# Opening of a two-model transformer kernel: products of zeros in the waits, squares summed half by half, modulation pieces two chunks ahead

## The chip, the cores and the metric

The kernel runs on one core of one Trainium2 chip, in one launch. The metric is the device time of a run in microseconds; lower is better. A core has five engines that run their own instruction lists and meet through semaphores: TensorE (PE) multiplies matrices, VectorE (DVE) and ScalarE (ACT) work element by element, GpSimd (POOL) does element work and issues transfers, SyncE (SP) issues transfers.

## The reference

A float32 network for one sequence of 256 tokens and a context of 256 tokens, width 1024. Two layers of a first model (feed-forward, mixing, feed-forward, each behind an RMS norm that is modulated by shift and scale) and two layers of a second model follow. The change touches only what precedes the first feed-forward product:

```python
def rms_norm(x, gain=None):
    xf = x.astype(jnp.float32)
    y = xf * lax.rsqrt(jnp.mean(xf * xf, axis=-1, keepdims=True) + EPS)
...
def modulate(h, shift, scale):
    return h * (1.0 + scale) + shift
def swiglu(h, w1, w3, w2):
    return (jax.nn.silu(h @ w1) * (h @ w3)) @ w2
```

Shift and scale are slices of silu(c) @ w_mod + b_mod for the tokens, and of silu(c_ctx) @ w_mod + b_mod for the context. For the first norm these are 2 x 1024 columns of the first layer's w_mod.

## The kernel before, in words

Activations are kept transposed: 8 chunks of 128 channels on the partitions, 512 columns (256 tokens of x, then 256 of the context). Every float32 weight is multiplied as a high and a low part. A "unit" is 128x1024 of weights. Six ring slots take units from HBM; ScalarE copies a unit rounded into `high` (line 1363, four slots), VectorE subtracts that from it into `low` (line 1864), and `product` (lines 808 to 810) makes three products per 128x128 block. `split_ahead` in both engines' lists keeps the splitting up to four units ahead of TensorE.

The opening (`start_units`) runs as follows.

- POOL issues x in two halves, the context in two halves, then the eight 1 MB pieces of `w_mod_first` (line 726, four slots; piece c holds the shift and scale columns of chunk c) with ring units 0 and 1 behind piece 0 and ring unit 2 behind piece 2. From piece 4 on it waits until TensorE has read the piece four before. SP issues units 3 and on when piece 7 has landed.
- ScalarE squares x and context, four chunks at a time (line 1806). VectorE adds eight chunks of squares to one in three steps per half (lines 2554, 2557, 2560), and TensorE sums them over the partitions with one product per half (lines 937 and 942) into the bank `means`. ScalarE takes the inverse root (lines 1370, 1373).
- For each chunk c: `first_modulation(c)` (line 906, 16 records) multiplies piece c; `first_rows(c)` copies the result out of PSUM on ScalarE (line 1782); `first_turn(c)` (line 915) sums and turns it into columns; `first_shift_scale(c)` (line 2524) and `first_scaled(c)` (line 2536) on VectorE; `first_high(c)` (line 1792) on ScalarE; `first_low(c)` (line 2546) on VectorE. Then `part(i, c)` multiplies chunk c into unit i, i being 0, 1 or 2.

The order is written out by hand in each engine's list. TensorE has: modulation c, part(2, c - 3), turn c, part(0, c - 1), part(1, c - 1). ScalarE has: rows c, high c, with the splitting of unit 2 behind high 1. VectorE has: shift and scale c, scaled c, low c, again with the splitting of unit 2 behind chunk 1. Behind the eight chunks comes the rest of the first feed-forward, a plain loop over units.

Of the kernel before, what the change touches and what calls it, by code (L numbers as in the profile page):

```python
# [32 lines left out]
ALU = mybir.AluOpType  # L33
# [25 lines left out]
FIRST_SLOTS = 4  # L59

# [158 lines left out]
def build(nc, A, old=None):  # L219
    ev = Events(*(old or (None, None)))  # L220
    ctx = ExitStack()
    with ctx:
# [101 lines left out]
        fresh = sb("fresh", 2 * N1).rearrange("p (b n) -> p b n", b=2)  # L324
        narrow = sb("narrow", N2 + 8 * NARROW)
# [282 lines left out]
        def _(pool):  # L608
# [114 lines left out]
            for c in range(KC):  # L723
                if c >= FIRST_SLOTS:
                    pool.wait_ge(*when("first_mod", c - FIRST_SLOTS))
                pool.dma_start(first_mod[:, c % FIRST_SLOTS], A["w_mod_first"][c].rearrange("p (k n) -> p k n", k=KC)).then_inc(
                    *made(f"first_mod_loaded{c % FIRST_SLOTS}", c, by=16))
                for s in ((0, 1), (), (2,))[c] if c < 3 else ():
                    pool.dma_start(ring[:, s], A["stream"][s]).then_inc(*made(f"first_unit_loaded{s}", s, by=16))
# [45 lines left out]
        def _(pe):  # L775
# [123 lines left out]

            def first_modulation(c):  # L900
# [18 lines left out]
            def start_units(tag, keys, xh, xl):  # L919
# [4 lines left out]
                def part(i, c):  # L924
# [9 lines left out]
                means = take("mean", ("start",))  # L934
                pe.wait_ge(*when("consts_loaded", 0))
                pe.wait_ge(*when("first_sums", 0))
                pe.matmul(means[:, 0:NX], cst(C_ONESD), sumsq[:, 0:NX], start=True, stop=True)
                pe.wait_ge(*when("c_cols_silu", 0))
                first_modulation(0)
                first_turn(0)  # L940
                pe.wait_ge(*when("first_sums", 1))
                pe.matmul(means[:, NX:N1], cst(C_ONESD), sumsq[:, NX:N1], start=True, stop=True).then_inc(
                    *made("mean", ("start",)))
                for c in range(1, KC):
                    first_modulation(c)
                    if c >= 3:
                        part(2, c - 3)
                    first_turn(c)
                    part(0, c - 1)
                    part(1, c - 1)  # L950
                pe.wait_ge(*when("consts_loaded_rest", 0))
                for i, c in ((2, 5), (0, 7), (1, 7), (2, 6), (2, 7)):
                    part(i, c)
# [393 lines left out]
        def _(act):  # L1347
# [463 lines left out]
            inverse_root(rstd[:, 0], bank("mean", ("start",)), N1, ("start",), ("mean", ("start",)))  # L1811
            first_high(0)
            split_ahead(1)
            for c in range(1, KC):
                first_rows(c)
                first_high(c)
                if c == 1:
                    split_ahead(1)
# [34 lines left out]
        def _(dve):  # L1853
# [661 lines left out]

            dve.memset(c_wide, 0.0).then_inc(*made("c_wide_cleared"))
# [34 lines left out]
            for g in range(2):  # L2551
                a, b = norm_cols(("start",), g)
                dve.wait_ge(*when("first_squares", g, 1))
                dve.tensor_tensor(scaled[:, 0:4, a:b], scaled[:, 0:4, a:b], scaled[:, 4:8, a:b], ALU.add).then_inc(
                    *made("first_sum_steps", "first_fours", g))
                dve.wait_ge(*when("first_sum_steps", "first_fours", g))
                dve.tensor_tensor(scaled[:, 0:2, a:b], scaled[:, 0:2, a:b], scaled[:, 2:4, a:b], ALU.add).then_inc(
                    *made("first_sum_steps", "first_twos", g))
                dve.wait_ge(*when("first_sum_steps", "first_twos", g))
                dve.tensor_tensor(sumsq[:, a:b], scaled[:, 0, a:b], scaled[:, 1, a:b], ALU.add).then_inc(  # L2560
                    *made("first_sums", g))
# [6 lines left out]
            for c in range(1, KC):  # L2568
# [3 lines left out]
                if c == 1:  # L2572
                    split_ahead(1)
# [173 lines left out]
```

## Time and profile before

| | |
|---|---|
| median of 3 runs | 2410.36 us (2410.29 to 2411.43) |
| the profiled execution, its own time | 2411.78 us |
| its span | 2409.5 us |
| TensorE busy | 2354.6 us (98%) |
| VectorE busy | 1537.7 us (64%) |
| ScalarE busy | 1012.7 us (42%) |
| GpSimd busy | 402.2 us (17%) |
| HBM read | 357.34 MB |

The profile is of one execution. Its span runs from the first to the last instruction; the time of the run is a little longer. In the timeline a row gives the start in us, the duration in us, engine, line, operation, what is written and read, and how often; brackets give the idle time of the engine before it and what ended that. PEld is TensorE's weight load, which overlaps its products. Ends of products are modelled, so consecutive ones overlap in the rows; their starts tell the pace.

### The profile page before, as it was taken

Reading aid. Unit: us, or ns where it says so; the run is one execution under the profiler, and the core shown is the slowest. Engines: PE = TensorE matmul, PEld = TensorE weight load, DVE = VectorE, ACT = ScalarE, POOL = GpSimd, SP = SyncE. Lnnn points to the kernel's source line nnn. Section 1 sums busy time; section 2 is a strip of 40 time slices with the busy share of each in tenths; the row PEclk is TensorE's granted clock in tenths of the full one; section 3 lists DMA queues with packets and bytes.
Section 4 is the critical chain, followed back from the end, with each engine's and each line's share of the span. In section 5 each row is a group of like instructions: output and inputs, shape, how many; then the busy total and the mean of one; then the engine's idle time right before and its main releaser. Section 6 shows DMA issues by size and latency. Waiting matters only on the chain.

```text
span 2409.5 us, 36413 instructions
## 1 busy us (share of the span) xinstructions
PE 2354.6 (98%) x14350; PEld 2038.1 (85%) x14350; DVE 1537.7 (64%) x2616; ACT 1012.7 (42%) x1690; POOL 402.2 (17%) x425
## 2 busy tenths in 40 slices
PE   7999999999999999999999999999999999999998
PEld 4888888777888888888888877999888999899887
DVE  5888775884698865523323585766666665667874
ACT  5222224645522223422223465555445444446663
POOL 2221211240122221111011131121000120000110
PEclk9999999999999999999999999999999999999999
DMA  8555542112366664222222222555433555434553
GB/s 341 193 208 207 186 158 90 62 53 93 114 219 235 238 217 157 88 96 97 96 97 99 87 80 76 188 184 188 156 106 127 172 175 175 148 117 152 190 189 135
DMA packets 97864, 360.75 MB, mean 150 GB/s; under 512 B 11024, under 2 KB 11792, under 8 KB 96544
## 3 DMA queue, kind: packets, MB, share of 16 engines
q1 hardware_dynamic: 75744, 272.84, 32.6%
q0 software_dynamic: 21952, 85.59, 9.8%
q8 instruction: 115, 1.88, 0.3%
q14 instruction: 53, 0.43, 0.1%
HBM read 357.34 MB, written 1.05 MB: 149 GB/s over the span
## 4 chain that ended last, share of the span: by engine, by line
PE 90%; DVE 3%; ACT 3%; issue 2%; DMA 1%; POOL 0%; DVEq 0%; ACTq 0%; POOLq 0%
PE bank L808 25%; PE bank L810 24%; PE bank L809 24%; PE bank L815 6%; PE bank L816 3%; PE bank L1143 1%; ACT ring_high L1363 1%; PE bank L1131 1%; PE bank L1113 1%; DVE ring_low L1864 1%; PE bank L1165 1%; PE bank L1092 0%; DMA arena<-w_mod_first_dram 0%; PE bank L1312 0%; PE bank L906 0%
## 5 line engine op out<-in xcount | busy, mean ns | idle before, releaser
L1864 DVE TENSOR_TENSOR ring_low<-ring,ring_high 128x1024 fp32r<-128x1024 f32 x520 | 641.2, 1234 | 509.1 <-ACT ring_high L1363 506.7
L808 PE MATMUL bank<-x_parts,ring_high 128*128 128x512 f32 (+2 forms) x2308 | 801.8, 347 | 6.9 <-DVE x_parts L1939 3.7
L1363 ACT ACTIVATE ring_high<-ring 128x1024 fp32r<-128x1024 f32 x520 | 547.9, 1054 | 582.0 <-PE bank L810 541.9
L810 PE MATMUL bank<-x_parts,ring_low 128*128 128x512 f32 (+2 forms) x2308 | 788.1, 341 | 0.0
L809 PE MATMUL bank<-x_parts,ring_high 128*128 128x512 f32 (+2 forms) x2308 | 786.6, 341 | 0.0
L808 PEld LDWEIGHTS bank<-x_parts,ring_high 128*128 128x128 f32 x2308 | 436.4, 189 | 73.6 <-issue 14.4
L809 PEld LDWEIGHTS bank<-x_parts,ring_high 128*128 128x128 f32 x2308 | 436.8, 189 | 47.0 <-issue 1.0
L810 PEld LDWEIGHTS bank<-x_parts,ring_low 128*128 128x128 f32 x2308 | 436.3, 189 | 47.6
L640 POOL TENSOR_TENSOR hidden_parts<-fresh,hidden_parts 128x512 fp32r<-128x512 f32 (+2 forms) x132 | 205.0, 1553 | 1013.1 <-ACT hidden_parts L1496 1013.1
L1877 DVE CUSTOM_DVE_ANT_0 mod_products<-mod_ring,csilu 128x1024 bf16<-128x1024 f32 x224 | 300.9, 1379 | 30.5 <-DMA mod_ring<-w_mod_dram 29.6
L808 PE MATMUL bank<-hidden_parts,ring_high 128*128 128x512 f32 (+2 forms) x814 | 280.9, 345 | 0.8 <-POOL hidden_parts L640 0.8
L810 PE MATMUL bank<-hidden_parts,ring_low 128*128 128x512 f32 (+2 forms) x814 | 280.1, 344 | 0.0
L809 PE MATMUL bank<-hidden_parts,ring_high 128*128 128x512 f32 (+2 forms) x814 | 280.1, 344 | 0.0
L808 PEld LDWEIGHTS bank<-hidden_parts,ring_high 128*128 128x128 f32 x814 | 153.6, 189 | 19.5 <-POOL hidden_parts L640 1.3
L809 PEld LDWEIGHTS bank<-hidden_parts,ring_high 128*128 128x128 f32 x814 | 153.6, 189 | 18.1
L810 PEld LDWEIGHTS bank<-hidden_parts,ring_low 128*128 128x128 f32 x814 | 153.6, 189 | 18.1
L1485 ACT ACTIVATE act_out<-bank 128x512 f32<-128x512 f32 x66 | 39.5, 599 | 264.6 <-PE bank L810 264.6
L815 PE MATMUL bank<-x_parts,ring_high 128*128 128x512 f32 x352 | 123.2, 393 | 0.0
L815 PE MATMUL bank<-hidden_parts,ring_high 128*128 128x512 f32 x308 | 106.9, 392 | 0.0
L808 PE MATMUL bank<-early_parts,ring_high 128*128 128x258 f32 x352 | 99.9, 284 | 0.0
L810 PE MATMUL bank<-early_parts,ring_low 128*128 128x258 f32 x352 | 99.3, 282 | 0.0
L809 PE MATMUL bank<-early_parts,ring_high 128*128 128x258 f32 x352 | 99.3, 282 | 0.0
(264 smaller groups left out, 2738.5 us busy)
## 6 DMA issues: line engine op xcount, KB each, us to landing
ring<-stream_dram SPq DMA_DIRECT2D x517, 512.0 KB, 3.3
mod_ring<-w_mod_dram POOLq DMA_DIRECT2D x128, 512.0 KB, 4.4
arena<-w_mod_first_dram POOLq DMA_DIRECT2D x8, 1024.0 KB, 10.3
ring<-stream_dram POOLq DMA_DIRECT2D x3, 512.0 KB, 10.8
arena<-na_bias_dram POOLq DMA_DIRECT2D x2, 768.0 KB, 11.0
mod_ring<-consts_dram POOLq DMA_DIRECT2D x1, 1076.0 KB, 5.1
resid<-x_dram POOLq DMA_DIRECT2D x2, 512.0 KB, 6.0
resid<-ctx_dram POOLq DMA_DIRECT2D x2, 512.0 KB, 7.2
```

The source lines that it names most:

```text
L640: pool.tensor_tensor(lo[:, f], fresh[:, f % 2, 0:n], hi[:, f].bitcast(F32), ALU.subtract).then_inc(*made("hidden_low", tag, h, f))
L808: pe.matmul(out, w[0][:, b], xh, start=start, stop=False)
L809: pe.matmul(out, w[0][:, b], xl, start=False, stop=False)
L810: return pe.matmul(out, w[1][:, b], xh, start=False, stop=stop)
L815: pe.matmul(bank.rearrange("p (k n) -> p k n", k=2), w[0][:, b], both, start=start, stop=False)
L816: return pe.matmul(bank[:, 0:NX], w[1][:, b], high, start=False, stop=stop)
L1113: mm = pe.matmul(out, pr["q"][r, q:q + nq], pr["k"][r, 0:NZ if twin else nk], start=not fox, stop=True, skip_group_check=nq < P)
L1131: mm = pe.transpose(p[0:rows, kt * P:kt * P + nq], probs[0:nq, b, e, kt * P:kt * P + rows], cst(C_IDENT, nq, nq))
L1363: act.activation(high[:, i % SPLIT], ring[:, u % LOADED], ACT.Copy).then_inc(high_parts, 1)
L1485: act.activation(act_out[:, f % 2, 0:n], p[:, 0:n], ACT.Silu).then_inc(*made("silu", tag, h, f, frees=("gate", tag, h, f)))
L1864: dve.tensor_tensor(low[:, u % LOADED], ring[:, u % LOADED], high_f[:, i % SPLIT], ALU.subtract).then_inc(low_parts, 1)
L1877: dve.tensor_tensor_reduce(junk[:, s], mod_ring[:, n % MOD_RING], csilu[:, s], 1.0, 0.0, ALU.mult, ALU.add, mod[:, l, s, j:j + 1]).then_in ...
```

## The change

`zeros` is the second half of `fresh[:, 1]`, set to zero by VectorE's first instruction. `idle_products(count, key)` waits for an event and then multiplies zeros by zeros into bank 4, `count` times. They are put ahead of and between the sums and the first two modulations. The squares are added from four chunks to two on VectorE, one add for each half and each four chunks, and TensorE sums the remaining pairs itself, eight products accumulated in `means`. On TensorE modulation and turn run two chunks ahead of the parts, and `first_rows` on ScalarE moves accordingly; the splitting of unit 2 moves behind chunk 2. Ring unit 1 is issued behind piece 1 and ring unit 2 behind piece 3.

```diff
--- before.py
+++ after.py
@@ -57,6 +57,7 @@
 LN_EXP = "natural_log_exp_and_others"
 
 FIRST_SLOTS = 4
+IDLE_BANK = 4
 
 
 
@@ -322,6 +323,7 @@
         act_out = sb("act_out", 2 * N1).rearrange("p (b n) -> p b n", b=2)
         c_wide = act_out[:, 0, 0:KC * 32].rearrange("p (c n) -> p c n", c=KC)
         fresh = sb("fresh", 2 * N1).rearrange("p (b n) -> p b n", b=2)
+        zeros = fresh[:, 1, NX:N1]
         narrow = sb("narrow", N2 + 8 * NARROW)
         row_scale = narrow[:, 0:N2]
         gate_w = narrow[:, 16:16 + 16 * NARROW].rearrange("p (s b n) -> p s b n", s=2, b=8)
@@ -725,7 +727,8 @@
                     pool.wait_ge(*when("first_mod", c - FIRST_SLOTS))
                 pool.dma_start(first_mod[:, c % FIRST_SLOTS], A["w_mod_first"][c].rearrange("p (k n) -> p k n", k=KC)).then_inc(
                     *made(f"first_mod_loaded{c % FIRST_SLOTS}", c, by=16))
-                for s in ((0, 1), (), (2,))[c] if c < 3 else ():
+                if c in (0, 1, 3):
+                    s = min(c, 2)
                     pool.dma_start(ring[:, s], A["stream"][s]).then_inc(*made(f"first_unit_loaded{s}", s, by=16))
             pool.dma_start(resid[:, :, 0:META], A["meta"]).then_inc(*made("meta_loaded", 0, by=16))
             pool.dma_start(const[:, C_ONES64:CONSTS], A["consts"][:, C_ONES64:CONSTS]).then_inc(
@@ -897,6 +900,13 @@
                         for c in order:
                             part(i, c)
 
+            def idle_products(count, *ready):
+
+
+                pe.wait_ge(*when(*ready))
+                for _ in range(count):
+                    pe.matmul(psum[IDLE_BANK][:, 0:NX], zeros[:, 0:P], zeros, start=True, stop=True)
+
             def first_modulation(c):
 
                 p = take_at(5 + c % 2, "first_rows", c)
@@ -932,25 +942,47 @@
                         mm.then_inc(*made(*keys[i], unit=i))
 
                 means = take("mean", ("start",))
+
+                def sums(g, i):
+                    a, b = norm_cols(("start",), g)
+                    pe.wait_ge(*when("first_sums", g, i))
+                    for j in range(2):
+                        mm = pe.matmul(means[:, a:b], cst(C_ONESD), scaled[:, 4 * i + j, a:b],
+                                       start=(i == 0 and j == 0), stop=(i == 1 and j == 1))
+                    return mm
+
+                idle_products(7, "zeros_set")
+                idle_products(2, "x_loaded0", 0)
                 pe.wait_ge(*when("consts_loaded", 0))
-                pe.wait_ge(*when("first_sums", 0))
-                pe.matmul(means[:, 0:NX], cst(C_ONESD), sumsq[:, 0:NX], start=True, stop=True)
+                sums(0, 0)
+                idle_products(1, "ctx_loaded0", 0)
+                sums(0, 1)
+                sums(1, 0)
                 pe.wait_ge(*when("c_cols_silu", 0))
+                idle_products(1, "ctx_loaded1", 1)
                 first_modulation(0)
+                sums(1, 1).then_inc(*made("mean", ("start",)))
                 first_turn(0)
-                pe.wait_ge(*when("first_sums", 1))
-                pe.matmul(means[:, NX:N1], cst(C_ONESD), sumsq[:, NX:N1], start=True, stop=True).then_inc(
-                    *made("mean", ("start",)))
+                idle_products(2, "first_mod_loaded0", 0)
+                first_modulation(1)
+                idle_products(1, "first_mod_loaded1", 1)
+                first_turn(1)
+                part(0, 0)
+                first_modulation(2)
+                part(1, 0)
+                first_turn(2)
                 for c in range(1, KC):
-                    first_modulation(c)
-                    if c >= 3:
-                        part(2, c - 3)
-                    first_turn(c)
-                    part(0, c - 1)
-                    part(1, c - 1)
+                    part(0, c)
+                    part(1, c)
+                    if c + 2 < KC:
+                        first_modulation(c + 2)
+                    if c >= 2:
+                        part(2, c - 2)
+                    if c + 2 < KC:
+                        first_turn(c + 2)
                 pe.wait_ge(*when("consts_loaded_rest", 0))
-                for i, c in ((2, 5), (0, 7), (1, 7), (2, 6), (2, 7)):
-                    part(i, c)
+                part(2, KC - 2)
+                part(2, KC - 1)
 
             def begun(prev):
 
@@ -1809,12 +1841,15 @@
             split_ahead(1 - SPLIT)
             act.wait_ge(*when("mean", ("start",)))
             inverse_root(rstd[:, 0], bank("mean", ("start",)), N1, ("start",), ("mean", ("start",)))
+            first_rows(1)
             first_high(0)
             split_ahead(1)
+            first_rows(2)
             for c in range(1, KC):
-                first_rows(c)
                 first_high(c)
-                if c == 1:
+                if c + 2 < KC:
+                    first_rows(c + 2)
+                if c == 2:
                     split_ahead(1)
             for l in range(DEPTH):
                 t1, tm, to, t2 = ("ffn1", l), ("mix1", l), ("out1", l), ("ffn2", l)
@@ -2513,6 +2548,7 @@
                     if k < len(PROJ2):
                         project(tp, PROJ2, k, N2, proj2, VTEMP2)
 
+            dve.memset(zeros, 0.0).then_inc(*made("zeros_set"))
             dve.memset(c_wide, 0.0).then_inc(*made("c_wide_cleared"))
             dve.memset(eps_one[:, 0:1], EPS).then_inc(*made("eps_one", 0))
             dve.memset(eps_one[:, 1:2], 1.0).then_inc(*made("eps_one", 1))
@@ -2550,15 +2586,10 @@
 
             for g in range(2):
                 a, b = norm_cols(("start",), g)
-                dve.wait_ge(*when("first_squares", g, 1))
-                dve.tensor_tensor(scaled[:, 0:4, a:b], scaled[:, 0:4, a:b], scaled[:, 4:8, a:b], ALU.add).then_inc(
-                    *made("first_sum_steps", "first_fours", g))
-                dve.wait_ge(*when("first_sum_steps", "first_fours", g))
-                dve.tensor_tensor(scaled[:, 0:2, a:b], scaled[:, 0:2, a:b], scaled[:, 2:4, a:b], ALU.add).then_inc(
-                    *made("first_sum_steps", "first_twos", g))
-                dve.wait_ge(*when("first_sum_steps", "first_twos", g))
-                dve.tensor_tensor(sumsq[:, a:b], scaled[:, 0, a:b], scaled[:, 1, a:b], ALU.add).then_inc(
-                    *made("first_sums", g))
+                for i in range(2):
+                    dve.wait_ge(*when("first_squares", g, i))
+                    x = scaled[:, 4 * i:4 * i + 4, a:b]
+                    dve.tensor_tensor(x[:, 0:2], x[:, 0:2], x[:, 2:4], ALU.add).then_inc(*made("first_sums", g, i))
             dve.wait_ge(*when("small_loaded", 0))
             first_shift_scale(0)
             split_ahead(1 - SPLIT)
@@ -2569,7 +2600,7 @@
                 first_shift_scale(c)
                 first_scaled(c)
                 first_low(c)
-                if c == 1:
+                if c == 2:
                     split_ahead(1)
             split_ahead(1)
             for l in range(DEPTH):
```

## Rows read from the trace of the kernel before

**Rows 1.** Page: the chain that ended last, shares of the span by engine.

```profile
PE 90%; DVE 3%; ACT 3%; issue 2%; DMA 1%; POOL 0%; DVEq 0%; ACTq 0%; POOLq 0%
```

**Rows 2.** Waits of TensorE from 50 us on: total, times, longest.

```profile
PE bank L1281 <- DVE fresh L2134: 4.4, 2, 2.3
```

**Rows 3.** Windows: busy us and instructions of each engine, granted clock, DMA share, GB/s.

```profile
12.00:28.80 16.80, 12.75 (x66) 6.41 (x66) 10.16 (x18) 7.32 (x13) 1.21 (x3) 1.00 1.01 416
28.80:54.00 25.20, 24.66 (x172) 17.10 (x173) 15.30 (x42) 10.62 (x20) 7.08 (x13) 1.00 0.91 353
54.00:90.00 36.00, 36.00 (x160) 29.84 (x159) 32.05 (x42) 14.71 (x20) 9.82 (x9) 1.00 0.56 203
```

**Rows 4.** Timeline, end of the opening: start, us, engine, line, operands, idle before.

```profile
49.69 0.88 DVE L2546 SCALAR_TENSOR_TENSOR x_parts<-arena,mod,x_parts 128x256 fp32r<-128x256 f32 x2 [0.24 <-ACT x_parts L1792]
...
50.72 0.47 PE L808 MATMUL bank<-x_parts,ring_high 128*128 128x512 f32 x1 [0.42 <-DVE x_parts L2546]
...
53.56 0.39 PE L808 MATMUL bank<-x_parts,ring_high 128*128 128x512 f32 x1
```

**Rows 5.** Timeline, modulation 2, while slow.

```profile
26.39 1.94 PE L906 MATMUL bank<-arena,act_out 128*32 128x256 f32 x16
```

**Rows 6.** Timeline, one chunk (4) once fast.

```profile
34.65 1.07 PE L906 MATMUL bank<-arena,act_out 128*32 128x256 f32 x16
...
35.79 0.38 ACT L1782 ACTIVATE fresh<-bank 128x256 f32<-128x256 f32 x1 [0.65 <-PE bank L906]
...
36.83 0.48 PE L808 MATMUL bank<-x_parts,ring_high 128*128 128x512 f32 x1
...
37.00 0.35 DVE L2524 TENSOR_SCALAR mod<-bank,small 128x2 f32<-128x2 f32 x2 [1.34 <-PE bank L915]
...
37.97 0.91 ACT L1792 ACTIVATE x_parts<-arena,mod 128x256 fp32r<-128x256 f32 x2 [1.80 <-DVE arena L2536]
...
38.39 1.07 PE L906 MATMUL bank<-arena,act_out 128*32 128x256 f32 x16
...
38.51 0.89 DVE L2546 SCALAR_TENSOR_TENSOR x_parts<-arena,mod,x_parts 128x256 fp32r<-128x256 f32 x2 [0.24 <-ACT x_parts L1792]
```

**Rows 7.** Timeline, 10 to 14 us.

```profile
10.79 0.69 DVE L2557 TENSOR_TENSOR arena<-arena 128x512 f32<-128x512 f32 x1
11.27 1.06 ACT L1806 ACTIVATE arena<-resid 128x1024 f32<-128x1024 f32 x1 [0.36 <-DMA resid<-ctx_dram]
...
12.09 1.19 PE L937 MATMUL bank<-sumsq,const 128*128 128x256 f32 x2 [12.09 <-DVE sumsq L2560]
...
13.86 1.94 PE L906 MATMUL bank<-arena,act_out 128*32 128x256 f32 x16 [0.58 <-DMA arena<-w_mod_first_dram]
```

**Rows 8.** Timeline, 18 to 30 us.

```profile
18.40 0.69 ACT L1370 ACTIVATE rstd<-bank,eps_one 128x512 f32<-128x512 f32 x1 [1.22 <-PE bank L942]
...
18.80 1.93 PE L906 MATMUL bank<-arena,act_out 128*32 128x256 f32 x16 [0.44 <-DMA arena<-w_mod_first_dram]
...
19.86 0.88 DVE L2536 SCALAR_TENSOR_TENSOR arena<-resid,mod,rstd 128x256 f32<-128x256 f32 x2 [0.96 <-ACT rstd L1373]
...
23.55 0.77 PE L808 MATMUL bank<-x_parts,ring_high 128*128 128x512 f32 x1
...
25.50 1.04 ACT L1363 ACTIVATE ring_high<-ring 128x1024 fp32r<-128x1024 f32 x1
...
26.58 1.23 DVE L1864 TENSOR_TENSOR ring_low<-ring,ring_high 128x1024 fp32r<-128x1024 f32 x1 [0.46 <-ACT ring_high L1363]
...
29.36 0.47 PE L808 MATMUL bank<-x_parts,ring_high 128*128 128x512 f32 x1
```

**Rows 9.** Timeline of TensorE around its longest idle time but one.

```profile
1723.03 0.63 PE L1281 MATMUL bank<-fresh,mod_ring 128*8 128x272 f32 x2 [2.10 <-DVE fresh L2134]
...
1723.82 0.29 PE L809 MATMUL bank<-x_parts,ring_high 128*128 128x272 f32 x1
1723.94 0.28 PE L810 MATMUL bank<-x_parts,ring_low 128*128 128x272 f32 x1
```

## The prediction, written before the result was known

> **What bounds the kernel now.** I read the page's chain of waits first, then the busy shares, then the waits of TensorE after the opening. The chain lies on TensorE for 90% of the span [rows 1], and behind 54 us it stands still only in small pieces, the largest group being 4.4 us [rows 2]. From 54 to 90 us it is busy without a break [rows 3]. VectorE is nearly full there too (32.05 of 36 us), but it splits a weight unit some units before TensorE multiplies it, so it doesn't set the pace. No row shows anything there that waits for a fixed time. So whatever the opening wins or loses reaches the end one for one, and the question is when TensorE leaves the opening. Before, the first product of unit 3, which follows the last of the opening, starts at 53.56 [rows 4].
>
> The opening itself has two parts. [...] From 29 us on it is busy for 24.66 of 25.2 us: each chunk costs 3.74 us (modulation of one chunk starts at 34.65, of the next at 38.39) [rows 6], and that is TensorE's own work.
>
> **The start, up to the first product of chunk 1.** On VectorE three adds per half, in a row, go (the middle one took 0.69 us [rows 7], the first has twice its size, the last half of it) and two of the middle size per half come, so VectorE has less to do. The last square ends at 11.27 + 1.06 = 12.33 [rows 7], so its add ends near 13.1. Added on TensorE: eight products of 128x256 for the sums in place of two, and 14 products of zeros. A product of this form appears as two records, 1.19 us with its tail when cold [rows 7]; I take 0.85 us apart when cold, 0.43 warm. The memset of zeros has the size of one that is there for `c_wide`; it delays ScalarE's table loads by some tenths, and the squares wait for their transfers well behind those (the last starts at 11.27 [rows 7]), so it costs nothing. The first nine idle products run from 1.3 to between 7 and 9 us, beside the transfers of x; the sums of the first three halves and their two fillers fit before 13.9 if the clock is up by then (three sums of 0.87, two fillers of 0.43; the last starts at about 11.8). I take it that it is up: nine products without a gap are some 7 us of work, and in the trace the clock was still low at 26.39 and came up behind that, after products that began at 23.55 [rows 5, 8].
>
> Then, with the clock up:
> - Modulation 0 still waits for its transfer, at 13.86 [rows 7]. ScalarE copies its rows 1.14 us behind it (34.65 to 35.79 [rows 6]), 15.0, and splits unit 0 (1.04 for such a split [rows 8]) until 16.4. The last sum (0.87) ends at 15.8, hidden by that. The root starts at 16.4, where it was 18.40, and 1.46 us later (18.40 to 19.86 [rows 8]) VectorE scales chunk 0: 17.9.
> - Modulation 1 is loaded earlier: one ring unit (0.52 MB) is now behind it in POOL's queue, at the 416 GB/s of this stretch [rows 3] 1.3 us, so at 17.5 in place of 18.80 [rows 8]. Here the first cost appears: `first_rows(1)` stands ahead of `first_high(0)` on ScalarE, so it waits for modulation 1: 17.5 + 1.14 = 18.64, and high 0 starts at 18.9, not at 18.4. Low follows 0.54 later (37.97 to 38.51), and the first product 1.03 behind the low's start (49.69 to 50.72) [rows 4, 6]: 20.5, before 23.55 [rows 8].
> - Unit 1 is split on ScalarE from 19.8 and on VectorE from 20.9 to 22.1; only then comes shift 1, with 0.97 from it to the high (37.00 to 37.97), then low and product: the first product of chunk 1 at 24.6. Before: 29.36 [rows 8]. So 4.8 us are won here.
>
> Queues that the edit passes: ring unit 1 lands where modulation 1 did, 18.8, for a split at 19.8: 1 us of cover, and what is lost of it moves chunk 1. Ring unit 2 is at about 25, needed at 32. Modulations 4 to 7 are issued as their slots come free, earlier than before; modulation 4 by bytes (5.8 MB behind piece 0 at 416 GB/s) at 27.7, needed at 30.8; later ones have more room. SP's stream starts when piece 7 has landed, sooner than before; unit 3 is needed only behind 53, so this is worth nothing.
>
> **The loop over the chunks.** TensorE's order is now: two groups of products of chunk c (units 0 and 1), modulation c + 2, the third unit's group of chunk c - 2, turn c + 2. The work is the same 3.7 us. But ScalarE's order is high c, rows c + 2, high c + 1, and rows in the trace come in program order. So high c + 1 waits for modulation c + 2, which TensorE starts only behind its groups of chunk c, which need low c. That closes a loop: groups 0 and 1 of a chunk until the modulation starts, 1.56 us (36.83 to 38.39); modulation to rows 1.14; rows to the next instruction 0.3; high to low 0.54; low to product 1.03 [rows 4, 6]. Sum 4.57 us per chunk, against 3.74. Behind the modulation TensorE has 1.0 + 0.89 + 0.34 of work and then stands for about 0.8 us. Before, high c waited for modulation c in the same way, but behind that modulation TensorE still had both groups of chunk c - 1 to do, some 1.5 us, and these covered it.
>
> At chunk 2 it is worse. The split of unit 2 follows rows 4, so it too waits for modulation 4; VectorE waits for it behind low 2, and shift, scale and low of chunk 3 queue behind. From modulation 4: 1.14 + 0.3 + split to low split 1.08 (25.50 to 26.58 [rows 8]) + its own 1.15 + shift to high 0.97 (37.00 to 37.97 [rows 6]) + 0.54 + 1.03 = 6.2, with the 1.56 before it 7.8 us from chunk 2 to chunk 3. TensorE stands for some 2.8 us of it before the third unit's first group. Before, this split sat in the slow stretch, ahead of modulation 2.
>
> Sum from the first product of chunk 1: 4.57 (to 2) + 7.75 (to 3) + 3 x 4.57 (to 6) + 2.4 (to 7, where no modulation is left: VectorE's own round of a chunk, 0.88 for the low, then 0.97 + 0.54 [rows 6]) + the five groups left, 15 products at 0.23 (TensorE's 12 from 50.72 to 53.56 give 0.237 [rows 4]) = 3.5. That is 31.9 us, where before it took 53.56 - 29.36 = 24.2. Lost here: 7.7. Won before: 4.8. TensorE leaves the opening at 56.5 instead of 53.6, **3.0 us later**.
>
> [...] No row here shows an instruction passing another.
>
> **Against the runs.** The profiled execution took 2411.78 us (span 2409.5), the median 2410.36. So 2414.8 profiled, and by the median 2413.4. 3.0 us are 0.12%; 0.2% (4.8 us) is about what can be told from no change.
>
> **Rivals.**
> - *The clock doesn't come up early* (9 us of products of zeros aren't enough). Then they only stand in the way: nine at 0.85 until 9.0, sums and fillers until 15.9, modulation 0 at 15.9 instead of 13.86, the sum in front of the turn 1.7, three more fillers 2.6, modulations at 1.94. The first product of chunk 1 comes near 31, at worst 1.7 later than before, and with the 7.7 of the loop that is +9.2: 2419.6. It decides if the clock rises behind 16 us (from there the loss is over 5). For it: from 12 to 28 us a TensorE with 12.75 us of work in 16.8 stayed slow [rows 3]. Against it: that work was broken by waits again and again, and the first nine products of zeros follow each other without one. A part of it is a clock that falls again in the 2.8 us stand of chunk 2; against that, products behind an idle time of 2.10 us still come 0.12 us apart, at 272 columns the fast level [rows 9]. It would add 1 to 3 us. [...]
> - *The loop is hidden and the start's gain stays*: TensorE bound at 3.74 from 24.6: 24.2 us on, end at 48.8, -4.8 us, 2405.6. It needs high c + 1 not to wait for rows c + 2. The code's order excludes it nearly; a half way case (delays shorter than I read them, 0.3 us per chunk, and the split of unit 2 landing in the loop) gives -1 to +1.
> - *The transfers set the start*: pieces 1 and 2 land 1.3 us later than by bytes (my bound is the old 18.80). Then chunk 1 is 1.3 us later: +4.3, 2414.7.
>
> **Chances.** Forecast with its own range of +1 to +4.7: 0.62. Slow clock, wholly or in part: 0.17, nearly all of it above +4.8 us. Hidden loop or half way: 0.13, of which 0.07 is beyond -4.8 us. Late transfers: 0.08, half of it above +4.8. Of the forecast's own 0.62 some 0.04 lies above too. Faster by over 0.2%: 0.07; within: 0.69; slower: 0.24. The range leaves out the wholly hidden loop and a little of the cold case: 2409.0 to 2419.5.
>
> **What would show it.** Idle products from 1.3 us, their records 0.43 apart in the start at first, then 0.2; modulation 0 at 13.9 lasting 1.07; scale of chunk 0 at 17.9; first product at 20.5, of chunk 1 at 24.6. In the loop: ScalarE's high always directly behind rows, modulations 4.6 us apart for pieces 5 to 7, TensorE idle 0.8 us before each first group and 2.8 us at 32, ended by VectorE's low part. First product of unit 3 at 56.5. I am wrong if modulations come 3.7 us apart, or if the sixteen products at 13.9 still take 1.9 us.

## The result, and the profile after

The changed kernel took 2417.19 us in the median of 11 runs (2414.21 to 2419.87), the kernel before 2410.74 in the 11 runs beside it (2409.95 to 2413.45): +6.4 us, ratio 1.0023, 95% interval 1.0015 to 1.0030. The prediction was 2413.4 with a range of 2409.0 to 2419.5. So the time lies in the range and on the side forecast, but the loss is twice the 3.0 us of the sum, and above the forecast's own +1 to +4.7. The profiled execution took 2414.21 (span 2412.0) and is the fastest of the eleven; that matters below. One run of the kernel before in a slow state (2911.7 us at a granted clock of 0.753, beside the f experiments) is left out of every figure.

The start went as worked out. First the timeline of TensorE in the changed kernel up to the first product of chunk 1, whose counterpart before was at 29.36 [rows 8]:

```profile
1.19 7.00 PE L908 MATMUL bank<-fresh 128*128 128x256 f32 x18 [1.19 <-DVE fresh L2551]
...
13.84 1.07 PE L916 MATMUL bank<-arena,act_out 128*32 128x256 f32 x16 [0.64 <-DMA arena<-w_mod_first_dram]
...
17.61 1.07 PE L916 MATMUL bank<-arena,act_out 128*32 128x256 f32 x16 [0.32 <-DMA arena<-w_mod_first_dram]
...
20.58 0.47 PE L811 MATMUL bank<-x_parts,ring_high 128*128 128x512 f32 x1 [0.73 <-DVE x_parts L2582]
...
24.57 0.47 PE L811 MATMUL bank<-x_parts,ring_high 128*128 128x512 f32 x1 [0.82 <-DVE x_parts L2582]
```

The 18 records in the first row are nine products of zeros, 7.0 us. Modulation 0 lasts 1.07 us, where it lasted 1.94 [rows 7]: the clock is up. Chunk 0 starts at 20.58 (20.5 forecast), chunk 1 at 24.57 (24.6).

Then the loop and the stand (the long wait of TensorE at chunk 2), first on TensorE and then on ScalarE (start, us, engine, what):

```profile
26.13 1.07 PE L916 MATMUL bank<-arena,act_out 128*32 128x256 f32 x16
...
29.11 0.47 PE L811 MATMUL bank<-x_parts,ring_high 128*128 128x512 f32 x1 [0.73 <-DVE x_parts L2582]
...
30.65 1.07 PE L916 MATMUL bank<-arena,act_out 128*32 128x256 f32 x16
...
34.42 0.80 PE L811 MATMUL bank<-x_parts,ring_high 128*128 128x512 f32 x1 [2.71 <-DVE ring_low L1899]
35.02 0.63 PE L812 MATMUL bank<-x_parts,ring_high 128*128 128x512 f32 x1
...
36.82 0.77 PE L811 MATMUL bank<-x_parts,ring_high 128*128 128x512 f32 x1
...
39.64 1.64 PE L916 MATMUL bank<-arena,act_out 128*32 128x256 f32 x16
...
44.75 1.07 PE L916 MATMUL bank<-arena,act_out 128*32 128x256 f32 x16
...
49.26 1.07 PE L916 MATMUL bank<-arena,act_out 128*32 128x256 f32 x16
...
54.54 0.47 PE L811 MATMUL bank<-x_parts,ring_high 128*128 128x512 f32 x1
...
58.05 0.39 PE L811 MATMUL bank<-x_parts,ring_high 128*128 128x512 f32 x1
```

```profile
31.78 0.38 ACT L1814 ACTIVATE fresh<-bank 128x256 f32<-128x256 f32 x1 [3.34 <-PE bank L916]
32.06 1.05 ACT L1395 ACTIVATE ring_high<-ring 128x1024 fp32r<-128x1024 f32 x1
...
45.88 0.39 ACT L1814 ACTIVATE fresh<-bank 128x256 f32<-128x256 f32 x1 [3.34 <-PE bank L916]
46.16 0.90 ACT L1824 ACTIVATE x_parts<-arena,mod 128x256 fp32r<-128x256 f32 x2
```

The second fence is ScalarE: the split of unit 2 starts right behind rows 4, and a high right behind rows 6, each after 3.34 us of waiting for TensorE's modulation. TensorE in turn stands 0.73 us before a chunk and 2.71 us before the third unit's first group, released by unit 2's low part. Modulations are 4.52 us apart from chunk to chunk (26.13 to 30.65, 44.75 to 49.26), against 3.74 before [rows 6]. All this is the forecast. What isn't: the row at 35.02 takes 0.63 us and the modulation at 39.64 takes 1.64. The clock has fallen in the stand. The windows say it too (us, busy time of PE, PEld, DVE, ACT, POOL, granted clock, DMA share, GB/s):

```profile
28.80:54.00 25.20, 20.08 (x124) 13.45 (x125) 11.18 (x32) 6.80 (x16) 5.45 (x11) 0.86 0.88 348
33.00:35.00 2.00, 0.58 (x1) 0.50 (x2) 1.82 (x4) 0.11 (x1) 1.25 (x3) 0.76 1.02 334
35.00:37.00 2.00, 1.90 (x8) 1.64 (x7) 1.68 (x6) 0.91 (x2) 0.00 (x0) 0.50 0.99 386
37.00:39.00 2.00, 2.00 (x5) 1.60 (x6) 0.98 (x3) 0.00 (x0) 0.00 (x0) 0.50 1.02 407
```

In the first of these stretches the clock before was 1.00 [rows 3]. (The column says 1.00 from 12 to 28.8 us before as well, where modulation 2 takes 1.94 us [rows 3, 5]; there only the durations show that TensorE is slow.) At a granted clock of 0.50 the products of 512 columns start 0.43 us apart (37.38 to 37.81), at 1.00 they start 0.23 us apart (29.41 to 29.64). Chunk 3 started at 36.82 and chunk 4 at 43.21: 6.4 us in place of 4.6. The last chunk starts at 54.54, five groups of three products follow, and the first product of unit 3 comes at 58.05, before at 53.56 [rows 4]: 4.5 us later in this execution, where 3.0 were forecast. From the first product of chunk 1 the chunks take 4.5, 7.7, 6.4, 4.5, 4.5 and 2.3 us and the five groups 3.5; the forecast's terms were 4.57, 7.75, three times 4.57, 2.4 and 3.5. One term is off by more than 0.1 us, that of the slow stretch, by 1.8.

The span is only 2.5 us longer. The lag of 4.5 us holds until 633 us; behind that the clock falls in both executions now and then (granted 0.83 from 630 to 640 and from 1410 to 1420 us before, 0.83 from 1000 to 1010 and 0.81 from 1726 to 1735 in the changed kernel), and TensorE waited 0.7 and 0.6 us less at two places that the change doesn't touch.

### The profile page after: what moved, and what is told of

Read it like the earlier page. It is cut to its first block, busy times and chain, and to the rows that moved or that the text cites. A ratio compares the mean times of both kernels' runs of the same rounds, so it can differ in the third digit from the quotient of the medians.

```text
span 2412.0 us, 36492 instructions
## 1 busy us (share of the span) xinstructions
PE 2364.8 (98%) x14390; PEld 2047.0 (85%) x14390; DVE 1535.9 (64%) x2615; ACT 1012.6 (42%) x1690; POOL 400.3 (17%) x425
## 4 chain that ended last, share of the span: by engine, by line
PE 89%; DVE 4%; ACT 3%; issue 2%; DMA 1%; POOL 0%; DVEq 0%; ACTq 0%; POOLq 0%
PE bank L811 25%; PE bank L813 24%; PE bank L812 24%; PE bank L818 6%; PE bank L819 3%; ACT ring_high L1395 1%; PE bank L1175 1%; DVE ring_low L1899 1%; PE bank L1163 1%; PE bank L1145 1%; PE bank L1197 1%; DMA arena<-w_mod_first_dram 0%; PE bank L1124 0%; PE bank L1344 0%; DVE arena L1965 0%
```

## The experiments

Each was timed beside the kernel before, in three groups: e1, e2, e3 and e5 (median of before 2411.40), e4, e6, e7 and e8 (2411.94), and f1 to f4 (2411.64). The table gives the difference from that median and the ratio with its 95% interval, which is some 2 us to either side for eleven runs. A difference between two kernels of the table is therefore sure to some 2.7 us (an estimate: two such intervals, added as squares). The last column is the start of the first product of unit 3, the first behind the opening, in the profiled execution (before: 53.56).

| kernel | median, us | against before, us | ratio | unit 3, us |
|---|---|---|---|---|
| changed | 2417.19 | +6.4 | 1.0023 (1.0015 to 1.0030) | 58.05 |
| e1_split_first | 2410.94 | -0.5 | 1.0000 (0.9991 to 1.0008) | 52.96 |
| e2_high_first | 2407.01 | -4.4 | 0.9986 (0.9977 to 0.9994) | 49.41 |
| e3_fill_stand | 2414.18 | +2.8 | 1.0015 (1.0006 to 1.0024) | 57.53 |
| e4_no_idle (5 runs) | 2421.21 | +9.3 | 1.0038 (1.0024 to 1.0052) | 63.13 |
| e5_idle_only | 2408.04 | -3.4 | 0.9989 (0.9981 to 0.9998) | 51.42 |
| e6_high_first_no_idle | 2409.26 | -2.7 | 0.9988 (0.9979 to 0.9997) | 50.80 |
| e7_old_order | 2410.05 | -1.9 | 0.9992 (0.9983 to 1.0000) | 50.95 |
| e8_squares_only | 2410.40 | -1.5 | 0.9993 (0.9984 to 1.0002) | 54.67 |
| f1_fill_gaps | 2407.16 | -4.5 | 0.9984 (0.9975 to 0.9992) | 49.43 |
| f2_old_order_ring | 2406.85 | -4.8 | 0.9984 (0.9975 to 0.9993) | 49.20 |
| f3_chunk1_early | 2406.47 | -5.2 | 0.9980 (0.9971 to 0.9989) | 49.15 |
| f4_high_first_split_late | 2411.33 | -0.3 | 1.0000 (0.9991 to 1.0008) | 53.40 |

**The stand: e1_split_first.** On ScalarE, against the changed kernel:

```diff
                 first_high(c)
+                if c == 2:
+                    split_ahead(1)
                 if c + 2 < KC:
                     first_rows(c + 2)
-                if c == 2:
-                    split_ahead(1)
```

> The changed kernel, with ScalarE's split of unit 2 ahead of rows 4 instead of behind them. My theory: the 2.7 us stand of TensorE at chunk 2 comes from that split waiting for modulation 4, and it also throws the clock down. Then chunk 2 to 3 costs 4.55 us like the others, the granted clock stays 1.00, and the first product of unit 3 starts at about 53.2 (57.4 in the changed kernel): -0.4 us against before, median about 2410.3. Rival (the loss sits in the transfers or behind the opening): stays at 2415 to 2417.

Measured 2410.94: as the theory says. The place of this split was worth 6.9 us (+6.4 against -0.5, each by its own before). In its timeline of ScalarE the split runs while ScalarE would wait anyway, and the chunks still come 4.5 us apart (rows 3 at 27.16, rows 4 at 31.70):

```profile
27.16 0.38 ACT L1814 ACTIVATE fresh<-bank 128x256 f32<-128x256 f32 x1 [3.36 <-PE bank L916]
27.44 0.90 ACT L1824 ACTIVATE x_parts<-arena,mod 128x256 fp32r<-128x256 f32 x2
28.23 1.04 ACT L1395 ACTIVATE ring_high<-ring 128x1024 fp32r<-128x1024 f32 x1
31.70 0.39 ACT L1814 ACTIVATE fresh<-bank 128x256 f32<-128x256 f32 x1 [2.42 <-PE bank L916]
```

**The loop: e2_high_first.** As the one before, and:

```diff
-                if c + 2 < KC:
-                    first_rows(c + 2)
+                if 2 < c + 1 < KC:
+                    first_rows(c + 1)
```

> As the one before, and on ScalarE high c + 1 ahead of rows c + 2 (the order is high 1, high 2, rows 3, high 3, rows 4, ...). My theory: ScalarE's order closes the loop of 4.55 us per chunk; with it opened TensorE is the bound at 3.73 us per chunk from 24.6 us on, unit 3 starts at about 48.8, -4.8 us against before, 2405.9. Rival (VectorE's chain or the transfers of the pieces set the pace of a chunk, not ScalarE's order): the chunks stay over 4.2 us apart and it ends within 1 us of the first experiment.

Measured 2407.01, -4.4: another 3.9 us. In the traces the five chunks from 1 to 6 take 18.6 us, where e1_split_first took 22.7, and the last one 0.4 us more: 3.7 us. ScalarE's timeline shows the loop open; the high of chunk 3 (29.39) waits for VectorE and stands ahead of rows 4 (30.96), which wait 0.66 us only:

```profile
27.28 0.38 ACT L1814 ACTIVATE fresh<-bank 128x256 f32<-128x256 f32 x1
29.39 0.91 ACT L1824 ACTIVATE x_parts<-arena,mod 128x256 fp32r<-128x256 f32 x2 [1.73 <-DVE arena L2572]
30.96 0.39 ACT L1814 ACTIVATE fresh<-bank 128x256 f32<-128x256 f32 x1 [0.66 <-PE bank L916]
```

**Loop open, stand kept: f4_high_first_split_late.** The same order, but unit 2's split behind rows 4; on ScalarE, against e2_high_first (and on VectorE `c == 3` for `c == 2`):

```diff
-                if c == 2:
-                    split_ahead(1)
                 if 2 < c + 1 < KC:
                     first_rows(c + 1)
+                if c == 3:
+                    split_ahead(1)
```

> The second experiment's order on ScalarE (high c + 1 ahead of rows c + 2), but unit 2's split left behind rows 4 (on VectorE behind low 3): the loop is opened, the stand is kept. From modulation 4 the third unit's first group has to wait 1.14 + 0.3 + 1.08 + 1.3 = 3.8 us, of which 1.0 is the modulation: TensorE stands 2.8 us once, and the later chunks cost 3.73. My theory: 2.8 to 4 us over the second experiment (the upper end if the clock falls in the stand), -0.5 to -1.6 against before. Rival (the stand's price is mostly in the chunks' loop behind it): within 1.5 us of the second experiment.

Measured -0.3, 4.1 over e2_high_first: the upper end. Its profile shows the stand alone, 2.71 us, and a fallen clock from 1 us behind its end (0.63 for the product at 36.05; granted 0.50 from 34.5 to 37.5, 1.00 again from 38). The two faults do not simply add: with the stand in place, opening the loop gained 6.8 us (changed kernel against this one), and without it 3.9. In the changed kernel the clock stayed at 0.50 from 35 to 39 us, and here it was up by 38.

```profile
32.00 1.23 DVE L1899 TENSOR_TENSOR ring_low<-ring,ring_high 128x1024 fp32r<-128x1024 f32 x1 [1.51 <-ACT ring_high L1395]
33.28 0.50 PE L811 MATMUL bank<-x_parts,ring_high 128*128 128x512 f32 x1 [2.71 <-DVE ring_low L1899]
...
36.05 0.63 PE L811 MATMUL bank<-x_parts,ring_high 128*128 128x512 f32 x1
```

**The clock in the stand: e3_fill_stand.**

```diff
+                    if c == 2:
+                        idle_products(5, "zeros_set")
                     if c >= 2:
                         part(2, c - 2)
```

> The changed kernel with five more products of zeros in the stand at chunk 2, ahead of the third unit's first group. The stand stays, as unit 2's low part comes no sooner; only TensorE isn't idle in it. My theory: the part of the loss beyond 3 us is the clock that falls in that stand, so with it filled the clock stays up and it takes about 2413.8, 3.1 over before, with less spread than the changed kernel. Rival (the idle time itself doesn't move the clock, or the spread is from elsewhere): 2417 as the changed kernel.

Measured +2.8 (2414.18), 3.7 less than the changed kernel when each is taken against its own before. Against e1_split_first, measured beside it, it is 3.2 us slower, which is the stand by the forecast's own terms (7.75 - 4.57). The time is what the theory gave. The profile doesn't give its reason as neatly: in this one execution the clock fell as well, for about 3 us (granted 0.50 from 31 to 33) and ahead of the stand, where TensorE had only the loop's pauses of 0.6 to 0.7 us. Modulation 4 is slow, and behind the products of zeros, from 35.74, the products are fast:

```profile
29.84 0.47 PE L811 MATMUL bank<-x_parts,ring_high 128*128 128x512 f32 x1
30.11 0.63 PE L812 MATMUL bank<-x_parts,ring_high 128*128 128x512 f32 x1
30.54 0.63 PE L813 MATMUL bank<-x_parts,ring_low 128*128 128x512 f32 x1
31.10 1.94 PE L916 MATMUL bank<-arena,act_out 128*32 128x256 f32 x16
32.96 2.64 PE L908 MATMUL bank<-fresh 128*128 128x256 f32 x10
35.74 0.50 PE L811 MATMUL bank<-x_parts,ring_high 128*128 128x512 f32 x1
```

So in this execution filling the stand left a short slow stretch; it doesn't keep the clock from falling each time.

**What products of zeros are worth: e4_no_idle, e6_high_first_no_idle, e5_idle_only.** The first two leave them out of the changed kernel and of e2_high_first (the waits stay); the third has nothing but them, added to the kernel before (below the edit of the first two, and of the third on TensorE).

```diff
-                for _ in range(count):
+                for _ in range(0):
```

```diff
+                idle_products(7, "zeros_set")
+                idle_products(2, "x_loaded0", 0)
+                idle_products(1, "ctx_loaded0", 0)
+                idle_products(1, "ctx_loaded1", 1)
                 pe.wait_ge(*when("consts_loaded", 0))
...
+                    if c == 1:
+                        idle_products(2, "first_mod_loaded0", 0)
                     first_modulation(c)
+                    if c == 1:
+                        idle_products(1, "first_mod_loaded1", 1)
```

> The changed kernel without its products of zeros; the waits that stood in front of them stay. My theory: the clock comes up only behind 23 us, modulations 0 and 1 and the sums take twice as long, the first product of chunk 1 comes at about 27.5 in place of 24.6, and the pauses of the loop make it fall or stay low for a part of the chunks too: +3 to +5 us over the changed kernel, 2420 to 2422. Rival (the start waits for transfers, the clock is of no account there): 2417 as the changed kernel.

> The second experiment (unit 2's split early, high c + 1 ahead of rows c + 2) without the products of zeros. If their worth is the same under any order, it takes 3 to 4 us more than the 2407.0 of the second experiment: 2410.5. Rival (with an order that has no pauses the clock comes up by itself nearly as soon): under 1.5 us more, 2408.5 at most.

> The kernel before with the products of zeros alone (14 of them, at the start, in front of and behind modulation 1); order, sums and transfers as before. My theory: the clock comes up before 14 us and that is worth nearly all that the start can win: modulation 2 at 22.6 in place of 26.4, then 3.73 us per chunk: -4.5 us, 2406.2. Rival (the start waits for the transfers and for the sums on VectorE, so a fast clock gives little): -1 us or less.

Without them the changed kernel takes 2421.21, 2.8 more against its own before and just under my +3 to +5, and e2_high_first 2409.26, 1.7 more by the same count (2.3 by the medians), between theory and rival. Neither difference is clear of its uncertainty. Half of my reason was wrong. In e4_no_idle modulation 0 runs fast already, behind the first six products of the sums and nothing else; the clock falls afterwards, in the pauses (granted 0.50 from 20 to 26 us):

```profile
13.95 1.07 PE L916 MATMUL bank<-arena,act_out 128*32 128x256 f32 x16
17.70 1.07 PE L916 MATMUL bank<-arena,act_out 128*32 128x256 f32 x16 [1.28 <-DMA arena<-w_mod_first_dram]
22.22 1.94 PE L916 MATMUL bank<-arena,act_out 128*32 128x256 f32 x16
```

Added to the kernel before they give -3.4, less than the 4.5 expected. In the profiled execution they didn't hold the clock up to modulation 0, with 2.4 us of waits for the context's transfers between them and only two products for the sums; modulations 0 and 1 ran slow, 2 fast, 1.6 us sooner than before [rows 5]:

```profile
13.95 1.93 PE L915 MATMUL bank<-arena,act_out 128*32 128x256 f32 x16 [0.60 <-DMA arena<-w_mod_first_dram]
20.08 1.94 PE L915 MATMUL bank<-arena,act_out 128*32 128x256 f32 x16
24.81 1.07 PE L915 MATMUL bank<-arena,act_out 128*32 128x256 f32 x16
```

**Squares alone: e8_squares_only.** The kernel before with VectorE's two adds per half and, on TensorE:

```diff
-                pe.wait_ge(*when("first_sums", 0))
-                pe.matmul(means[:, 0:NX], cst(C_ONESD), sumsq[:, 0:NX], start=True, stop=True)
+                sums(0, 0)
+                sums(0, 1)
+                sums(1, 0)
                 pe.wait_ge(*when("c_cols_silu", 0))
                 first_modulation(0)
+                sums(1, 1).then_inc(*made("mean", ("start",)))
                 first_turn(0)
-                pe.wait_ge(*when("first_sums", 1))
-                pe.matmul(means[:, NX:N1], cst(C_ONESD), sumsq[:, NX:N1], start=True, stop=True).then_inc(
-                    *made("mean", ("start",)))
```

> The kernel before with the squares summed half by half alone (two adds per half on VectorE, eight products on TensorE, the last two behind modulation 0). My theory: at the slow clock the three sums (1.7 us each) end at 14.1, modulation 0 starts 0.2 us later than before and the last sum takes 1.7 where 0.9 was; the root starts within 1 us of 18.4: -0.5 to +1 us, 2411 to 2412. Rival (more work on TensorE before 14 us brings the clock up by itself): -3 us.

Measured -1.5, with an interval that holds 1. Between theory and rival, and for the rival's reason: modulation 0 took 1.07 us at 13.78 here. It didn't last: in this execution, the slowest of its eleven, modulation 2 took 1.94 us at 24.30.

**Is running two chunks ahead worth anything? e7_old_order, f2_old_order_ring.** The changed kernel's start with the old order in the chunks on all three engines. On TensorE, the prologue of chunks 1 and 2 gone, it is again:

```diff
+                for c in range(1, KC):
+                    first_modulation(c)
...
+                    if c >= 3:
+                        part(2, c - 3)
+                    first_turn(c)
+                    part(0, c - 1)
+                    part(1, c - 1)
```

The second has the ring units issued as before too:

```diff
-                if c in (0, 1, 3):
-                    s = min(c, 2)
+                for s in ((0, 1), (), (2,))[c] if c < 3 else ():
```

> The changed kernel's start (products of zeros, squares half by half, ring units behind pieces 1 and 3) with the order of the kernel before in the chunks on all three engines. My theory: running two chunks ahead is worth nothing by itself, since TensorE is the bound at 3.73 us a chunk in both orders; the start is worth 4 us: modulation 2 at about 23, first product of unit 3 near 49.5, -4.1 us against before, 2407.2, the same as the second experiment. Rival (two chunks ahead helps once ScalarE's order is right): 2 us or more slower than the second experiment, 2409 or more.

> The experiment with the old chunk order, with the ring units issued as before too (0 and 1 behind piece 0, unit 2 behind piece 2). There ScalarE stood 1.8 us for ring unit 2, and rows 2 with turn 2 behind it. If that is why it missed the second experiment by 3 us, it now takes 1.5 us less, 3.5 under before. Rival (the old order loses by the clock that falls at chunk 0, as ring unit 2 only moves one wait into another): no less than 0.5 us better.

The first missed: 2410.05, -1.9, 2.5 us worse than e2_high_first by the same count, as the rival had it. Its profile named a wait, ScalarE's for ring unit 2, which the change moved behind piece 3; rows 2 stand behind that split:

```profile
24.85 1.06 ACT L1388 ACTIVATE ring_high<-ring 128x1024 fp32r<-128x1024 f32 x1 [1.81 <-DMA ring<-stream_dram]
25.82 0.36 ACT L1807 ACTIVATE fresh<-bank 128x256 f32<-128x256 f32 x1
```

With the old places of the ring units it takes 2406.85, -4.8, 2.9 better. That is more than the 1.5 of the wait; in the first the clock also fell behind 21.6 (granted 0.55 from 21.6 to 24), in the second's profile it didn't (1.00), so the rest may be clock. What follows: with each order's transfers right, two chunks ahead shows no gain over the order of before (f1_fill_gaps, measured beside it, is at -4.5).

**What is left: f1_fill_gaps, f3_chunk1_early.** One more product of zeros in each of the three pauses that e2_high_first has left (ahead of part(0, 0), of part(0, 1) and of turn 3), each `+ idle_products(1, "zeros_set")`; the second also has this, on ScalarE `first_high(1)` ahead of `first_rows(2)`, and on VectorE:

```diff
             first_low(0)
+            first_shift_scale(1)
+            first_scaled(1)
             split_ahead(1)
```

> The second experiment (unit 2's split early, high c + 1 ahead of rows c + 2) with one more product of zeros in each of the three pauses left: ahead of chunk 0's first product, ahead of chunk 1's, and ahead of turn 3. My theory: each is shorter than its pause (0.43 against 0.6 to 0.8 us), so nothing gets later, and the clock falls in fewer executions: 0.5 to 1 us under the second experiment, 4.5 to 5.4 under before. Rival (what is left of the spread has another cause): the same as the second experiment, within 0.5 us.

> The first of this call, and chunk 1's shift and scale on VectorE ahead of unit 1's low part, its high on ScalarE ahead of rows 2. My theory: chunk 1's first product starts 0.4 to 0.6 us sooner (at 24.1), TensorE is the bound from there, so 0.5 us under the first of this call, 5 to 6 under before. Rival (unit 1's low part, 0.9 us later, holds back its first group and turn 2 instead): no gain, or 0.3 us slower.

The first shows no gain (-4.5 against -4.4, and three of its eleven runs still have a granted clock of 0.994 and take 2410.3 to 2410.5). The second has the lowest median of all, 2406.47, -5.2; modulation 3 comes at 25.91 where f1_fill_gaps has 26.17. Its lead over its neighbours, 0.4 to 0.7 us, is inside their intervals. It beats both kernels.

## Why the prediction was right, and where its size was off

- *The opening decides, one for one.* Shown: every experiment changes the opening alone, and against before the median moves as the start of unit 3 does, within 1.3 us. Two are further off: the changed kernel (1.9), whose profiled execution is the fastest of its eleven, and e8_squares_only (2.6), whose is the slowest.
- *The start wins 4.8 us.* Shown: 29.36 to 24.57 in the profile, and f2_old_order_ring, which has no loop and starts chunk 1 at 25.02, 4.3 us sooner than before, is 4.8 under before. That the clock comes up through the products of zeros alone was wrong (e4_no_idle, e8_squares_only).
- *The loop of 4.57 us per chunk, closed by ScalarE's order.* Shown: 4.52 in the profile, and e2_high_first opens it for 3.9 us (3.7 in the traces).
- *The stand of 2.8 us.* Shown: 2.71 in the profile; e1_split_first takes it out, and f4_high_first_split_late puts it back into an open loop.
- *The sum, +3.0.* This is the term that was mis-sized: I priced the stand at its idle time and left the clock out of it. By the runs the stand cost 6.9 us (changed against e1_split_first, each with its own before), where the sum had 3.2 (7.75 - 4.57). Filling it with products of zeros gave back 3.7 of these without ending it sooner, and left +2.8, nearly the +3.0 of the sum. I had read the row of 2.10 us of idle time with fast products behind it [rows 9] as safety up to 2.8 us, and put the fall into a rival at 1 to 3 us with small weight. It belongs in the sum. One row was one draw, too: in the changed kernel's own trace the same wait, 2.15 us, has slow products behind it (last section). How much the clock costs depends on what follows the stand: with the loop open the stand cost 4.1 us (f4_high_first_split_late against e2_high_first).
- *The range.* That the time lies in it is in part luck. The forecast's own part went to +4.7 only; the range reached 2419.5 mainly for a clock that doesn't come up at the start, and in the profile it came up. (That rival's own sum was off as well: 1.7 + 7.7 is 9.4, not 9.2.)

The eleven runs of the changed kernel bear this out: those with a mean granted clock of 0.996 took 2414.2 and 2415.6 us, the one with 0.993 took 2419.9. 0.003 of 2415 us is 7.2 us of full clock lost (each of the two means is rounded), and the time differs by 5.0. The means over eleven runs say it for the unprofiled ones: 0.9946 in the changed kernel, 0.9965 in e1_split_first, which has the loop's pauses and no stand, and 0.9965 in e3_fill_stand. 0.0019 of 2415 us are 4.6 us of full clock, for the 3.7 us that filling the stand gave back. With the loop open the stand lowers it from 0.9964 to 0.9956.

In the changed kernel a high whose inputs are ready waits on ScalarE for the rows that stand ahead of it. VectorE scales chunk 2 in two halves from 24.72, the two take 0.88 us, and its high starts at 27.55, behind rows 3 at 27.27. In e2_high_first the same scaling starts at 24.75, no rows stand ahead of the high, and it starts at 25.33. The first case in the trace:

```profile
24.72 0.88 DVE L2572 SCALAR_TENSOR_TENSOR arena<-resid,mod,rstd 128x256 f32<-128x256 f32 x2
...
27.55 0.90 ACT L1824 ACTIVATE x_parts<-arena,mod 128x256 fp32r<-128x256 f32 x2
```

Open: a mean clock doesn't say where in an execution the clock was low. That the slow stretch of the unprofiled runs lies in and behind the stand is argued from one trace, from f4_high_first_split_late and from the times and means of e3_fill_stand and e1_split_first; no run shows how often it falls in the loop's pauses instead, as it did once in e3_fill_stand's trace.

## What to carry to other kernels

When work is moved ahead in one engine's list, follow it through the lists of the engines that answer it: here a copy placed one step too early on ScalarE closed a loop and cost 3.9 us, and a split behind it 6.9, more than all that the moved work had won. Price a stand of TensorE like this one, 2.7 us, at its idle time plus what the clock loses afterwards: here as much again with the pauses of the loop behind it (6.9 us in all), and some 1 us with the loop open (4.1 in all). A cheap run with the old order and the new start tells at once which half of a change pays.

## What the hardware showed that I had not expected

- The clock came up after few products: in e4_no_idle and e8_squares_only TensorE did six products of 128x256 between 8.8 and 13.9 us, and modulation 0 ran in 1.07 us; in the kernel before it did one, and modulation 0 took 1.94.
- Whether it falls differs between executions at the same place. It fell in a stretch without any idle time over 0.8 us (e3_fill_stand, between 24.6 and 30.1 us), where it stayed up in the changed kernel. Late in the kernel TensorE waits 2.1 to 2.3 us for VectorE: behind that the clock stayed up in the trace of before [rows 9] and in eight others, and fell in those of the changed kernel, e1, e2, e3 and f3. In the changed kernel the products of 272 columns behind it soon start 0.23 us apart, no longer 0.12:

```profile
1725.55 0.62 PE L1313 MATMUL bank<-fresh,mod_ring 128*8 128x272 f32 x2 [2.15 <-DVE fresh L2169]
...
1727.33 0.43 PE L813 MATMUL bank<-x_parts,ring_low 128*128 128x272 f32 x1
1727.56 0.43 PE L811 MATMUL bank<-x_parts,ring_high 128*128 128x272 f32 x1
```

The length of a single pause does not tell in these traces: the clock fell in the stand of 2.71 us, behind 2.15 us, and in e3_fill_stand with 0.8 us at most, and it stayed up behind 2.10 us in the kernel before [rows 9] and behind 2.17 us in e8_squares_only.
